# Moving the on-chip tiles of a two-block transformer kernel from 32 to 64 byte starts

## The reference, cut to what matters

```python
# first block, per layer: adaptive norm, two attentions, merge, swiglu
h = modulate(rms_norm(x, norm1_g[l]), sh1, sc1)
qa, ka, va, qb, kb, vb, ga, gb = split_in_proj(h @ w_in[l])
x = x + gt1 * merge_branches(ya, yb, ga, gb, w_proj_a[l], w_proj_b[l], w_out[l])
x = x + gt2 * swiglu(h2, w_ffn_gate[l], w_ffn_up[l], w_ffn_down[l])
# second block, per layer: one wide projection, three mixers, gated branches
p = h @ w_in
proj = jnp.einsum('bsgc,gcd->bsgd', branches, w_branch)
mixed = jnp.sum(gates * proj, axis=2)
x = x + (mixed @ w_out)
```

## The kernel before, in words

| tile | start before, modulo 64 | who reads it |
|---|---|---|
| `raw`, `high`, `low`, `vec` | 0 | splits, all products |
| `ones`, `square_sum`, `halves` | 32 | means, sums |
| `mean_d` / `mean_h` / `mean_64` | 0 / 32 / 0 | means (1 or 2 columns) |
| `few`, `xc`, `tmp`, `small`, `mod`, `gs`, `gfw` | 32 | norms, attention |
| `silu_c`, `col` | 0 | modulation |
| `cst2`, `cst`, `sq`, `hsq`, `hh`, `hl`, `ada_part` | 32 | constants, first block |
| gates, `K`, `V`, `Q`, `prob`, `probT`, `M`, `mt`, `hid`, `gt` | 32 | first block |
| `ukw`, `uvw`, `sq2`, `hsq2`, `hh2`, `hl2`, `sel`, `gcol` | 32 | second block |
| `ones4`, `lat`, `dqs`, `z`, `mg`, `x`, `SV`, `MV`, `hx`, `prob2`, `probT2`, `B`, `prod` | 0 | second block |

## Time and profile before

### The profile page before, as it was taken

One profiled execution on the slowest core, in us unless ns is written; L12 is line 12 of the kernel. 1 busy time (PEld: TensorE's weight loads), 2 busy tenths in 40 slices (PEclk: granted clock), 3 DMA queues, 4 the chain that ended last, 5 costly groups with the idle time before them and its releaser, 6 DMA issues.

```text
span 2082.3 us, 30759 instructions
## 1 busy us (share of the span) xinstructions
PE 1978.9 (95%) x12540; PEld 1637.1 (79%) x12540; DVE 1074.1 (52%) x2021; ACT 873.6 (42%) x1520; POOL 311.6 (15%) x149
## 2 busy tenths in 40 slices
PE   6999999999999999989989999899999899999996
PEld 3765576867888888677889999888788898788896
DVE  4335655632111111347766555569547755864675
ACT  3213445433222222324555444446454544755452
POOL 0220222433434444210000000000000000000100
PEclk9999999999999999999999999899999999999998
DMA  8333411244223222633247565443333444332341
GB/s 337 131 115 114 149 60 52 82 166 147 91 82 108 95 91 82 232 121 129 77 134 241 173 201 173 142 134 109 131 113 117 146 146 160 101 132 102 123 141 51
DMA packets 76700, 272.28 MB, mean 131 GB/s; under 512 B 8208, under 2 KB 11536, under 8 KB 76560
## 3 DMA queue, kind: packets, MB, share of 16 engines
q1 hardware_dynamic: 74656, 266.37, 37.8%
q10 hardware_dynamic: 1904, 3.94, 0.5%
HBM read 269.23 MB, written 1.05 MB: 130 GB/s over the span
## 4 chain that ended last, share of the span: by engine, by line
PE 83%; DVE 6%; ACT 5%; issue 2%; DMA 1%; POOL 1%; SPq 0%; ACTq 0%; DVEq 0%
PE bank L892 23%; PE bank L893 21%; PE bank L894 21%; PE bank L973 3%; PE bank L1053 2%; DVE low L1672 2%; PE bank L1084 2%; ACT high L1283 2%; PE bank L1066 2%; DMA raw<-stream 1%; PE bank L1014 1%; PE bank L1042 1%; PE bank L985 1%; POOL few L1615 1%; PE bank L1002 1%
## 5 line engine op out<-in xcount | busy, mean ns | idle before, releaser
L892 PE MATMUL bank<-h,high 128*128 128x256 f32 (+1 forms) x2432 | 800.7, 329 | 19.9 <-issue 6.8
L893 PE MATMUL bank<-h,high 128*128 128x256 f32 (+1 forms) x2432 | 765.0, 315 | 0.0
L894 PE MATMUL bank<-h,low 128*128 128x256 f32 (+1 forms) x2432 | 764.2, 314 | 0.0
L892 PEld LDWEIGHTS bank<-h,high 128*128 128x128 f32 x2432 | 466.2, 192 | 113.5 <-issue 71.5
L1283 ACT ACTIVATE high<-raw 128x1024 fp32r<-128x1024 f32 x408 | 426.7, 1052 | 216.7 <-PE bank L894 213.4
L894 PEld LDWEIGHTS bank<-h,low 128*128 128x128 f32 x2432 | 465.9, 192 | 29.5
L893 PEld LDWEIGHTS bank<-h,high 128*128 128x128 f32 x2432 | 466.6, 192 | 28.6 <-issue 1.7
L1672 DVE TENSOR_TENSOR low<-raw,high 128x1024 fp32r<-128x1024 f32 x296 | 364.2, 1233 | 231.2 <-ACT high L1283 230.2
L1606 POOL TENSOR_TENSOR low<-raw,high 128x1024 fp32r<-128x1024 f32 x112 | 272.0, 2435 | 504.3 <-ACT high L1283 504.3
L1615 POOL TENSOR_TENSOR few<-few,halves 128x2 f32<-128x2 f32 (+2 forms) x27 | 26.9, 998 | 826.5 <-DVE few L1758 826.5
L1699 DVE TENSOR_TENSOR gt<-bank,gt 128x512 f32<-128x512 f32 (+1 forms) x44 | 24.5, 557 | 202.9 <-PE bank L894 202.9
(11 more groups left out here) (280 smaller groups left out, 2536.0 us busy)
## 6 DMA issues: line engine op xcount, KB each, us to landing
raw<-stream SPq DMA_DIRECT2D x504, 512.0 KB, 3.3
xc<-x_in SPq DMA_DIRECT2D x1, 1024.0 KB, 5.7
xc<-ctx_in SPq DMA_DIRECT2D x1, 1024.0 KB, 8.2
out<-xc ACTq DMA_DIRECT2D x1, 1024.0 KB, 4.8
cst<-consts ACTq DMA_DIRECT2D x1, 896.0 KB, 6.2
cst<-consts ACTq DMA_DIRECT2D x1, 704.0 KB, 4.0
ukw<-uk ACTq DMA_DIRECT2D x1, 512.0 KB, 7.1
uvw<-uv ACTq DMA_DIRECT2D x1, 512.0 KB, 8.7
```

Of the source, the lines that this page charges most:

```text
L892: mm(dst, wh, xh, start=start, stop=False)
L893: mm(dst, wh, xl, start=False, stop=False)
L894: return mm(dst, wl, xh, start=False, stop=stop)
```

## The change

`vec` is rounded up from 276 to 288 columns (1104 to 1152 bytes) and used through its first 276. The three tables `gfw`, `col` and `gcol` are no longer tiles of their own but eight columns each of `small`, at columns 32, 40 and 48. Nothing else is edited: no instruction, wait, transfer or step is added, removed or moved.

```diff
-        vec = sb("vec", [P, VEC_N])
+
+        vec = sb("vec", [P, -(-VEC_N // 16) * 16])[:, 0:VEC_N]
...
         small = sb("small", [P, 64])
+        gfw, col, gcol = (small[:, 32 + 8 * i:40 + 8 * i] for i in range(3))
...
-        gfw = sb("gfw", [P, KT])
         silu_c = sb("silu_c", [P, KT, 32])
-        col = sb("col", [P, 8])
...
-        gcol = sb("gcol", [P, 8], scope=block2)
```

## The result

The changed kernel takes 2066.9 us, the median of 5 runs (2063.66 to 2069.08), where the kernel before, in 5 runs, takes 2078.62 us. The ratio, estimated from all of these runs and not from the two medians, is 0.9931, with a 95% interval of 0.9915 to 0.9946: faster by 0.5 to 0.9%, some 14 us (the medians lie 12 us apart). The forecast of 2086 us and its range from 2075 are both missed. The profiled execution has a span of 2062.2 us.

What follows compares the result with a forecast made beforehand. The kernel was taken as bound by TensorE's matmul pace. The narrow products gave +1.2 us and all else 0: 2085 us against the profiled execution, 2086.9 against the median, so 2086 us, range 2075 to 2093.

Steps and rivals of the forecast that it cites:

- What bounds the kernel, and that the edit costs nothing by itself: Whole kernel: TensorE's matmul pace reaches the end nearly one for one; no instruction, wait or transfer changes, only tile starts.
- 256-wide products: 6096 narrow matmuls: pace goes from 118.3 to B's 118.5 ns, +0.2 ns each, +1.2 us in all.
- starts modulo 128: Under the slower rival: h, B at 96, 0 before, 64 after, covered by no row; beyond 0.5% slower, 2096 us or more, 4%.
- 512-wide products: 2640 wide matmuls: pace 233.3 ns at starts 32 and 0 alike, so 0 us.
- Token stages: V's 192 matmuls whose stationary tile comes to 0: at most +0.3 us, taken as 0.
- Plain float32 matmuls, VectorE, ScalarE, weights' splits: Float32 matmuls, vector and scalar steps, splits: 0 us; the mean matmuls' 21 ns difference would be 2.3 us either way.
- A: 256-column products: alignment saves a 64-byte piece; V's pace gives 2076 us, 2067 with the 512-wide end; 11%.
- B's picture: Linear stages: two aligned streams begin in the same place and one waits; 2.3 us slower, 2088 us, 4%; beyond 0.5%, 4%.
- C: All matmul time above one cycle per column is the cost of starts at 32; 124 us would go, 1962 us; 3%.
- D: mean_d and mean_64 end at 32, so not every tile is aligned; 2.3 us either way, 2083 to 2088; within forecast's 78%.
- The page's rule: SBUF accesses pay at crossing a 16-byte line; 32 and 64 are both multiples, so by it alone time is unchanged.
- The list of signs: Profile after: hid should keep 31.1 and 61.4 us over 264 steps; other paces of hid or B would point to other causes.

Runs made afterwards that it cites:

- e10: The changed kernel with only the 512-column tiles (h, M, hid of layer 0) moved to a multiple of 256 bytes from the weights; 2056.12 us, ratio 0.9864.
- e1: The kernel before with only vec rounded up, the three tables left as tiles of their own; 2074.44 us, ratio 0.9962.
- e3: The changed kernel with 64 bytes of padding behind vec, so everything but the weights moves up by 64 bytes; 2076.82 us, ratio 0.9982.
- e7: The changed kernel with 512-column tiles at offset 0 from the weights and 256-column tiles at +112; 2053.25 us, ratio 0.9856.
- m2: Products alone on TensorE, on zeros, moving buffer shifted against the weights in 16-byte steps, some shifts of both; 272 to 288 cycles at 256 columns.
- m1: First kernel of products alone on TensorE, on zeros, moving and stationary tiles begun at chosen bytes; 272 cycles at offset -64 alone, in three of eight chains.
- m3: Products alone on TensorE, on zeros, both moving halves and the low weights at 0, 64, 128 or 192 bytes; 272 to 291 cycles at 256 columns.
- e8: The changed kernel again, unedited, on the same chip as the runs beside it; 2069.54 us, ratio 0.9935.
- e5: The changed kernel with 64 bytes of padding ahead of the first buffer, so weights, moving tiles and tables all move alike; 2066.78 us, ratio 0.9929.
- e6: The kernel before with only h2 moved, by 224 bytes, to the change's offset of -64 against the weights; 2073.07 us, ratio 0.9955.
- e9: e7 with h2 and B put back where the change has them, at -64 and +64; 2051.57 us, ratio 0.9845.
- e11: e7 repeated as comparison on the same chip; 2055.49 us, ratio 0.9868.

## Why the prediction was wrong

**What bounds the kernel, and that the edit costs nothing by itself: right.** TensorE kept its 95%, the busy time of VectorE, ScalarE and GpSimd moved by 1 us at most, and a change of pace went to the end nearly one for one (16 us in the steps, 14 in the time).

**The step that failed is the one on 256-wide products**, "I take it, because it is the same instruction with the same stationary tile and differs only in the moving tile's start". That one difference was put down as 32 or 0 modulo 64. It was -32 against 128 modulo 256, and the change brought neither, but -64. `B`'s 284.7 cycles were the pace of offset 128 and said nothing about the changed kernel. The term was put at +1.2 us and measured at -15.3 (`h2` -11.8, `h` and `hid` of layer 1 -2.6, `M` -0.9). The sentence on starts modulo 128, "that is where such a size could hide", named the hole, and the prediction then gave it 4%, and on the slow side only. With rows for two offsets and a third to come, both signs were as open. Of the 19 us between the forecast and the measured 2066.9, 12 are the change; the other 7 are the kernel before, whose median went from 2085.66 to 2078.62 us with two more runs.

**512-wide products: the number right, the reason wrong.** 0 us was forecast and 0.3 measured. But it was read as a sign that starts don't matter there. They do: 16 cycles less at offset 0, 17 us over the layer, of which e10 shows 11 to 13 us between its median and those of the changed kernel.

**Token stages:** V was put at 0 and went from 280 to 282.7 cycles, +0.2 us; SV and MV, not expected to move, gave 0.7 us, from 560 to 549.

**Plain float32 matmuls, VectorE, ScalarE, weights' splits:** nothing in the result asks for them. One reading was wrong: the tiles of both groups of mean matmuls in the earlier trace rows, `mean_d` and `mean_64`, begin at 0 in the kernel before, so these rows could not say whether the start orders them. The groups after, with both tiles at 32, do (`mean` is `mean_64`):

```profile
L1001 PE MATMUL bank<-mean,hsq 128*128 128x2 f32 x64 | 8.1, 244 | 2.5 <-ACT hsq L1353 2.5
L1001 PE MATMUL bank<-mean_d,square_sum 128*128 128x1 f32 x44 | 6.7, 268 | 9.3 <-DVE square_sum L1747 9.3
```

244 ns again and 268 for 265 are 0.1 us in sum, not 2.3. e2, which has only the tables moved, is level with the kernel before; there the tiles' offset moved as well, from -32 to -96, which in the steps without a gap is +2.4 us on the wide products and -3.4 us on the narrow ones of the linear stages, so that the two all but cancel (-1.5 us between the medians).

**The rivals.** A had the direction, and its 2067 us with the 512-wide end is the measured time by accident: its mechanism (a 64-byte piece more or less) fell in e1, e3 and e7, V, its evidence, got slower when its stationary tile became aligned too, and the 512-wide half of its sum did not come. B's picture, two streams that begin alike and meet, fits offset 0 at 256 columns (288 cycles in e1 and e3) and fails at 512, where the same offset is the fastest. C fell: the lowest paces anywhere are 113.3 and 226.7 ns. The first stays above the 109.2 ns that N / 2.4 + 2.5 gives for 256 columns on the page "TensorE: Matmul & The Clock Gate" of the Trainium skill, section "Back-to-back issue gap", which has this formula for an isolated matmul. D fell: its two tiles are worth the 0.1 us above.

**The page's rule** of 16-byte lines ("SBUF — State Buffer" of the Trainium skill, section "Specifications (TRN2)") gave no change. Offsets of 0, 64, 112 and 128 bytes are all whole multiples of 16, and alone on TensorE they have four paces at 256 columns, from 272 to 288 cycles; the measurement decides, and the rule can't stand for what two streams do to each other.

**The list of signs** had the right one: "if `B` [...] changes its pace as well, then it is the start modulo 128 or more that counts". `B` went from 118.5 to 117.8 ns.

## What to carry to other kernels

Before a row is taken as the case after the change, write down the full address of both operands and their difference, not the one property that the change names; a row at another difference is no evidence. Where TensorE is the bound and weights are loaded for each matmul, the place of the moving tiles against the weights is worth a map (a chain of products alone, in steps of 16 bytes, at each width), and each tile can have its own place. Compare traces step by step behind the start, and tell a pace that has two states from a gain.

## What the runs showed that was not expected

The pace of a float32r matmul whose weights are loaded beside the one before depends on the place of the moving tile against the weights: 272 to 288 cycles at 256 columns and 544 to 563 at 512 for the offsets in steps of 16 bytes, apart from two chains at 568, and the best offset for one width (0 for 512) is among the worst for the other. What in the chip makes it so was not shown.

At offset -64 the pace has two states, 272 and 282.7 cycles. It is set when a stretch begins and is held to its end. What sets it is open. Alone on TensorE, the chains behind two matmuls of 2 or of 1 column had 272 and those behind 128 or 256 columns 282.7 in m2, but with the weights moved up instead of the moving tile down, m1 had 282.7 behind 2, 128 and 1 column and 272 behind 256, and m3 had 282.7 behind both of its widths.

In the full kernel `M` of layer 1 had 272 in the profile of the change and 282.7 in e8, which is the same kernel. Most of `h2` is steadier: in the stretches of 13 steps and more, 272 took 87 to 91% of its steps in the three profiles of the change's layout (the change, e5, e8), and 56 to 59% in e6, e9 and e10, where `h2` has the same offset and other tiles stand elsewhere. So the offset makes the gain possible, and how much of it comes depends on something else that these runs don't name. The times of the runs with `h2` at -64 lie further apart (2063 to 2073 us in e8, 2044 to 2054 in e9) than those of e11 (2054.0 to 2055.9); but the mean granted clock goes with them (0.981 in the fastest of e8, 0.974 in the slowest), so how much of the spread is the two states isn't shown.
